# The first modulation third of a mixed attention, recurrence and expert layer, computed in two column halves

## The reference, cut to what matters

```python
def _modulation(cond, w, b):
    m = jax.nn.silu(cond) @ w + b
    return jnp.split(m[:, None, :], 6, axis=-1)

def _modulate(x, g, shift, scale):
    return _rmsnorm(x, g) * (1.0 + scale) + shift

proj = h @ p['w_in']          # h: the modulated x, 1024 features; w_in: 3232 columns
```

## Time and profile before

| | |
|---|---|
| three timed runs | 1644.02, 1645.7 and 1647.08 us; median 1645.7 |
| profiled execution, its own time | 1647.82 us |
| span of the profiled execution | 1646.0 us |
| granted TensorE clock, mean over the span | 0.956 of full |
| PE busy | 1508.4 us (92%) |
| DVE, ACT busy | 567.3 and 252.2 us |
| layer 1 starts (first ada product) | 839.23 us |
| DMA | 548.91 MB, mean 333 GB/s |

### The profile page before, as it was taken

The page is one execution under the profiler, slowest core; times in us unless marked ns, Lnnn a source line. Parts: engine busy times, 40 slices in busy tenths (PEclk is TensorE's granted clock), DMA queues, the critical chain, the costliest instruction groups (busy, mean ns, idle before and its releaser), DMA issues.

```text
span 1646.0 us, 19838 instructions
## 1 busy us (share of the span) xinstructions
PE 1508.4 (92%) x8048; PEld 886.4 (54%) x8048; DVE 567.3 (34%) x1463; ACT 252.2 (15%) x567; POOL 31.7 (2%) x30
## 2 busy tenths in 40 slices
PE   6999999989999989686899999999899999897878
PEld 2755788774454434242348567887744544343333
DVE  2368335435521112010144782363446112111112
ACT  2044122121000001000030442220200000000001
POOL 0000010020000000000000000100200000000000
PEclk7999999989999989798999999999899999999989
DMA  9743714787999999999996447228789999999995
GB/s 395 267 170 147 311 60 185 289 350 319 390 431 430 430 431 429 431 431 426 426 427 246 163 153 307 90 116 348 323 342 390 432 429 430 431 430 430 431 425 248
DMA packets 55914, 548.91 MB, mean 333 GB/s; under 512 B 13576, under 2 KB 14600, under 8 KB 21008
## 3 DMA queue, kind: packets, MB, share of 16 engines
q1 hardware_dynamic: 46416, 543.11, 79.2%
q10 hardware_dynamic: 9408, 4.53, 1.0%
HBM read 545.21 MB, written 2.42 MB: 333 GB/s over the span
## 4 chain that ended last, share of the span: by engine, by line
PE 74%; DMA 15%; DVE 6%; SPq 3%; issue 1%; ACT 0%; ACTq 0%; DVEq 0%
PE ps L782 19%; PE ps L1019 14%; PE ps L1049 10%; DMA arena<-exp_w_dram 8%; PE ps L743 7%; DMA ring<-exp_w_dram 5%; PE ps L960 5%; PE ps L1060 4%; PE ps L749 3%; PE ps L653 2%; SPq L484 2%; DMA ring<-front_dram 1%; PE ps L719 1%; PE ps L968 1%; PE ps L714 1%; PE ps L680 1%
## 5 line engine op out<-in xcount | busy, mean ns | idle before, releaser
L1019 PE MATMUL ps<-ring,arena 128*32 128x512 f32 (+2 forms) x1216 | 297.1, 628 | 41.9 <-DMA arena<-exp_w_dram 26.0
L1019 PE MATMUL ps<-arena 128*64 128x512 f32 (+1 forms) x896 | 231.9, 615 | 12.4 <-DMA ring<-exp_w_dram 12.4
L1019 PEld LDWEIGHTS ps<-ring,arena 128*32 128x32 f32 (+2 forms) x1216 | 90.4, 132 | 202.5 <-issue 194.6
L782 PE MATMUL ps<-hT,ring 128*128 128x256 f32 x768 | 171.4, 379 | 0.0
L1049 PE MATMUL ps<-ring,arena 128*32 128x512 f32 (+1 forms) x704 | 146.4, 622 | 16.8 <-DMA ring<-exp_w_dram 16.8
L782 PEld LDWEIGHTS ps<-hT,ring 128*128 128x128 f32 x768 | 144.1, 190 | 19.4 <-issue 1.0
L782 PE MATMUL ps<-arena,ring 128*128 128x256 f32 x640 | 147.0, 381 | 2.9 <-ACT arena L1243 1.6
L960 PE MATMUL ps<-arena,hT 128*128 128x128 f32 x896 | 120.6, 292 | 14.5 <-DVE arena L1755 14.5
L960 PEld LDWEIGHTS ps<-arena,hT 128*128 128x128 f32 x896 | 113.3, 205 | 35.7 <-DVE arena L1755 18.3
L782 PEld LDWEIGHTS ps<-arena,ring 128*128 128x128 f32 x640 | 117.8, 190 | 19.3 <-issue 2.7
L1019 PEld LDWEIGHTS ps<-arena 128*64 128x64 f32 (+1 forms) x896 | 67.5, 128 | 106.8 <-issue 106.8
(11 more groups left out here) (294 smaller groups left out, 1387.8 us busy)
## 6 DMA issues: line engine op xcount, KB each, us to landing
ring<-exp_w_dram SPq DMA_DIRECT2D x104, 2048.0 KB, 22.9
arena<-exp_w_dram SPq DMA_DIRECT2D x63, 2048.0 KB, 22.9
ring<-front_dram SPq DMA_DIRECT2D x58, 2048.0 KB, 10.3
arena<-exp_w_dram SPq DMA_DIRECT2D x24, 1024.0 KB, 29.1
ring<-exp_w_dram SPq DMA_DIRECT2D x16, 1024.0 KB, 13.7
ring<-exp_w_dram SPq DMA_DIRECT2D x24, 512.0 KB, 15.0
arena<-exp_w_dram SPq DMA_DIRECT2D x8, 512.0 KB, 29.5
ring<-front_dram SPq DMA_DIRECT2D x2, 1152.0 KB, 20.7
```

The costliest lines, as they stand in the source:

```text
L782: last = mm(out, slot[:, k, cols], src[:, k, :], start=k == 0, stop=k == nk - 1)
L1019: last = mm(ps[c, h, :], xTg[:, 4 * part + k, c], w[i][k][:, h * 512:(h + 1) * 512], start=False, stop=True, skip_group_check=True)
```

## The change

The first third is computed in two column halves. Half 0 takes columns 0 to 255 of each of the four groups of 512, half 1 columns 256 to 511. For shift and scale alike these are feature chunks 0, 1, 4, 5 and 2, 3, 6, 7, so everything that follows takes the chunks in the order `H_ORDER`. Each half has its own bank (0 and 1), its own copy on ACT (256 columns), its own two transposes (banks 3 and 4) and its own bias and `A1` operations on DVE.

In layer 0 PE takes each arriving ada block for both halves, then both pairs of transposes. In layer 1 PE does half 0 of all eight chunks, then the norm, the transposes of half 0, half 1 of all eight chunks, and then starts the input products; the transposes of half 1 stand inside unit 0, ahead of its third chunk. `ada_mm`, which frees the ring slots, is now raised by the products of half 1 alone.

On DVE the scaling and modulating of chunks alternate in layer 1, and the eight small operations come after all modulation. On ACT the softplus of layer 1 comes after the modulation. Two semaphores are merged and the counts adjusted.

```diff
+H_ORDER = (0, 1, 4, 5, 2, 3, 6, 7)
...
-                            sp_.wait_ge(*nth(ada_sb, 2, l))
+                            sp_.wait_ge(*nth(ada_sb, 3, l))
...
+                    def first_ada_products(half, slots):
+
+                        for k in (k for n in slots for k in (2 * n, 2 * n + 1)):
+                            slot = arrived(pe, l, S_ADA[0] + k // 2).rearrange("p (k n) -> p k n", k=2)
+                            for j in range(4):
+                                c = slice(j * 512 + half * 256, j * 512 + half * 256 + 256)
+                                last = mm(ps[32 * j:32 * j + 32, half, 0:256], cT[:, k, :], slot[:, k % 2, c],
+                                          start=k == 0, stop=k == KC - 1)
+                            if half and k % 2:
+                                last.then_inc(ada_mm, 1)
+                            if half == 0 and k == KC - 1:
+                                last.then_inc(ada_half, 1)
+
+                    def first_ada_transposes(half):
+                        pe.wait_ge(*nth(ada_sb, half + 1, l))
+                        for b in range(2):
+                            c = slice(half * 256 + b * P, half * 256 + (b + 1) * P)
+                            last = tr(ps[:, 3 + half, b * P:(b + 1) * P], msb[0][:, c], ident)
+                        last.then_inc(ada_tr, 1)
...
                     if l:
-                        ada_products(0, 0, range(KC // 2))
+                        first_ada_products(0, range(4))
                         norm(2)
-                        ada_products(0, 0, range(KC // 2, KC))
+                        first_ada_transposes(0)
+                        first_ada_products(1, range(4))
                     else:
                         norm(2)
                         pe.wait_ge(s_set[3], 4)
-                        ada_products(0, 0)
-                    ada_transposes(0, 3)
+                        for n in range(4):
+                            for half in range(2):
+                                first_ada_products(half, (n,))
+                        first_ada_transposes(0)
+                        first_ada_transposes(1)
...
-                                for k in range(KC):
+                                for i, k in enumerate(H_ORDER):
                                     if u == 0:
-                                        pe.wait_ge(*nth(h_v, k + 1, l))
+                                        if l and i == 2:
+                                            first_ada_transposes(1)
+                                        pe.wait_ge(*nth(h_v, i + 1, l))
...
+                    def first_modulation(half):
+                        if half == 0:
+                            act.wait_ge(*nth(ada_half, 1, l))
+                        else:
+                            act.wait_ge(*nth(ada_mm, 4, l))
+                        A(msb[0][:, half * 256:half * 256 + 256], ps[:, half, 0:256], ACT.Copy).then_inc(ada_sb, 1)
+
+                    def softplus():
+                        act.wait_ge(*nth(sp_abs, 1, l))
+                        link(A(sp[:, 8:16], sp[:, 0:8], ACT.Exp, scale=-1.0))
+                        A(sp[:, 16:24], sp[:, 8:16], ACT.Ln, bias=one_col).then_inc(ln_exp, 1)
+
+                    if l:
+                        first_modulation(0)
                     act.wait_ge(*nth(nrm_mm, 1, l))
                     A(rs[:, :], ps[:, 2, 0:NT], ACT.Sqrt, bias=cst[:, C_EPS:C_EPS + 1],
                       scale=1.0 / D).then_inc(nrm_sq, 1)
...
+                    if l == 0:
+                        softplus()
+                        first_modulation(0)
+                    first_modulation(1)
...
-                    for k in range(KC):
-                        act.wait_ge(*nth(hraw, k + 1, l))
+                    for i, k in enumerate(H_ORDER):
+                        act.wait_ge(*nth(mod_rdy, 1 + i // 4, l))
+                        act.wait_ge(*nth(hraw, i + 1, l))
...
+                    if l:
+                        softplus()
...
+                    if l:
+                        first_modulation(0)
                     dve.wait_ge(*nth(nrm_sq, 1, l))
                     link(V.reciprocal(rs[:, :], rs[:, :]))
-                    for k in range(KC):
-                        V.tensor_tensor(hT[:, k, :], xT[:, k, :], rs[:, :], ALU.mult).then_inc(hraw, 1)
-
+                    if l:
+                        scaled_x(H_ORDER[0])
+                        for i in range(4):
+                            scaled_x(H_ORDER[i + 1])
+                            modulate(i)
+                        for k in H_ORDER[5:]:
+                            scaled_x(k)
+                    else:
+                        for k in H_ORDER:
+                            scaled_x(k)
+                        first_modulation(0)
+                        for i in range(4):
+                            modulate(i)
+                    first_modulation(1)
+                    for i in range(4, 8):
+                        modulate(i)
```

More of the change, by code:

```diff
@@ L1372, in rsqrt, with modulation @@
                                                         op0=ALU.add, op1=ALU.mult))
+                    def modulation(r, bank):
+                        dve.wait_ge(*nth(ada_tr, r + 2, l))
+                        src = ps[:, bank, :].rearrange("p (b j z) -> p j b z", b=4, j=4)[:, :, :, 0:G]
+                        dst = modT[:, 16 * r:16 * r + 16, :].rearrange("p (j b) z -> p j b z", j=4)
+                        bias = vec[:, V_ADAB + 16 * r:V_ADAB + 16 * r + 16].rearrange("p (j b) -> p j b", j=4)
+                        link(V.tensor_tensor(dst, src, bias[:, :, :, None].broadcast_to((P, 4, 4, G)), ALU.add))
+                        if r == 1:
+                            V.tensor_scalar(g1h[:, :, :], modT[:, 16:24, :], 0.5, None, ALU.mult).then_inc(mod_rdy, 1)
+                        else:
+                            V.scalar_tensor_tensor(out=A2[:, :, :], in0=modT[:, 32:40, :], scalar=1.0,
+                                                   in1=vec[:, V_N2:V_N2 + 8][:, :, None].broadcast_to((P, KC, G)),
+                                                   op0=ALU.add, op1=ALU.mult).then_inc(mod_rdy, 1)
@@ new lines, in first_modulation @@
+                    def first_modulation(half):
+                        dve.wait_ge(*nth(ada_tr, half + 1, l))
+                        b = slice(2 * half, 2 * half + 2)
+                        src = ps[:, 3 + half, 0:256].rearrange("p (b j z) -> p j b z", b=2, j=4)[:, :, :, 0:G]
+                        dst = modT[:, 0:16, :].rearrange("p (j b) z -> p j b z", j=4)
+                        bias = vec[:, V_ADAB:V_ADAB + 16].rearrange("p (j b) -> p j b", j=4)[:, :, b]
+                        link(V.tensor_tensor(dst[:, :, b, :], src, bias[:, :, :, None].broadcast_to((P, 4, 2, G)), ALU.add))
+                        for j in range(2):
+                            k = 4 * j + 2 * half
+                            last = V.scalar_tensor_tensor(
+                                out=A1[:, k:k + 2, :], in0=modT[:, 8 + k:10 + k, :], scalar=1.0,
+                                in1=vec[:, V_N1 + k:V_N1 + k + 2][:, :, None].broadcast_to((P, 2, G)), op0=ALU.add,
+                                op1=ALU.mult)
+                        last.then_inc(mod_rdy, 1)
```

81 lines of the change are left out of this document (33 added, 48 removed).

## The result

The changed kernel takes 1650.33 us (median of 8 runs, 1649.18 to 1653.96), the kernel before 1646.34 (8 runs, 1643.61 to 1647.44): ratio 1.0025, 95% interval 1.0016 to 1.0035. It is slower by 4.0 us where +1.7 was forecast. The profiled execution took 1653.96 us, its span is 1652.1; it is the slowest of the eight, 3.6 us above their median.

A forecast was written before the change was run, and what follows sets the result against it. PE was taken to bound the kernel (three quarters of the chain), then DMA, saturated between layers. Terms -1.1 - 1.15 + 1.45 + 2.5 = +1.7 on 1645.7 gave 1647.4 us, no measurable change; range 1644.3 to 1650.0.

The forecast's parts named there:

- Layer 0, the start: Layer 0's start: last ada block lands at 28.5 either way, first input product at 33.9 against 35.00, -1.1 us.
- Layer 0, the clock: Layer 0's start: shorter PE idle time brings the full clock back at about 36.4 instead of 39.8, -1.15 us.
- middle: Layer 0's clock rise taken at about 36.4, between staying at 39.8 and coming before 33.9.
- Layer 1, the wait: Layer 1's ada products: PE waits 3.9 us for block 3, so the norm ends at 850.85, 4.4 us late.
- Layer 1, what is given back: Layer 1, after the norm: small operations leave the path, first input product at 855.1 against 853.68, net +1.45 us.
- the tie of DVE and PE: Layer 1's start: DVE allows the first input product at 854.8, PE's half 1 ends at 854.7.
- Layer 1, the clock: Layer 1, behind the wait for block 3: the clock falls to half rate, costing +2.5 us.
- Between: From layer 0's start on: PE has no hole worth the name until the experts, so a shift passes on; 0 us.
- the late blocks hidden: Layer 1: blocks 6 to 9 issued later, block 6 landing by about 865, needed at 873 or later; no cost.
- the signs named in the prediction: Among them: layer 0's first input product at 33.9; layer 1's 1 to 4 us later, counted from first ada product.
- the second one's other way: Slower side of the narrow-products rival: layer 0's clock gives nothing, layer 1's costs 2.85 us; chance 0.13 with that rival.
- The clock doesn't fall in layer 1: Rival for layer 1's start: clock stays full despite the wait; net -0.85 us, 1644.9 us, chance 0.10.

The follow-up runs named there:

- e2: Changed kernel with layer 1's order undone (blocks 0 and 1 for both halves, norm, blocks 2 and 3), halves kept: 1644.58 us, ratio 0.9995.
- b1: Kernel before with only the first third's products issued 256 columns wide, into two banks, order unchanged: 1650.77 us, ratio 1.0027.
- e3: Changed kernel with layer 1's norm moved between blocks 1 and 2 of half 0: 1646.33 us, ratio 0.9997.
- g3: g2 plus unread filler products of 512 columns where PE waits at the starts of both layers: 1650.55 us, ratio 1.0031.
- g4: g3 with fewer fillers, each of 256 columns: 1642.2 us, ratio 0.9973.
- e1: Changed kernel with nine unread products put on PE just ahead of layer 1's wait for block 3: 1648.67 us, ratio 1.0011.
- a1: Changed kernel, nothing altered, a third profile: 1651.48 us.
- g2: Kernel before with DVE's small operations moved behind the modulation, and in layer 1 ACT's softplus too; no products split: 1643.96 us, ratio 0.9988.
- p1: Kernel before, nothing altered, one more profile: 1647.89 us.

## Why the prediction was wrong

The means of the table's rows (four profiles of before, three of after) split the difference: to unit 4 of layer 0 54.93 and 55.38, +0.45; to layer 1 783.44 and 785.61, +2.2; layer 1's start 34.79 and 37.14, +2.35; the rest 773.20 and 773.17, nothing. Together +4.95 in these profiles, +4.0 in the medians of the timed runs. The forecast had -2.3, 0, +3.95, 0.

**Layer 0, the start: -1.1 forecast.** The step that failed is its first sentence, "the last ada block lands at 28.5 ... either way". The path behind the landing got shorter by 1.17 (forecast 1.1). But the block lands 1.5 us later, at 29.9 to 30.3 in all three profiles of the changed kernel and in both of e2 and of b1 (e3: 29.7). I had costed the 64 further products by their time on PE alone, which is nothing, and not as instructions that must themselves be loaded by the engines that carry the ring's blocks (the rows of queue 8 above: 3.0% of the 16 engines' time in those 2 us). b1, which adds only these products, has the earlier transfer and the later landing. g3, with 20 further products, has the transfer at 32.8, and there block 3 lands at 28.9 as before and block 4 is the late one (34.8 in place of 33.3); g4, with 13, has it at 36.6, behind blocks 3 and 4, which both land as before (28.5 and 33.4). Blocks 3 to 5 shift with it; from block 6 on the two kernels' blocks land alike (block 6 at 41.3 in both), since before has its transfer, and a like gap, ahead of that one. In layer 0 the link is one of place and time in every kernel looked at; that the transfer itself takes up 1.5 us of the stream, 0.02 MB though it is, was not isolated, and in layer 1 the link doesn't hold every time (below).

**Layer 0, the clock: -1.15 forecast.** Not obtained. The first 64 input products took 20.0, 20.1 and 20.3 us in the changed kernel and 20.7, 21.0, 20.0 and 20.0 before, so 0.3 on the mean. My "middle" between two ends had no row behind it. The clock there takes either way in like kernels: 18.35 in e1 and e2, 20.01 in e3.

**Layer 1, the wait: forecast 0.45 and 3.9 us,** norm's end 11.6 us behind the first ada product (839.23 to 850.85). Measured 1.77 and 3.79, norm's end at 15.6 (841.18 to 856.79). Of the 4.0 more, 1.5 is block 3, which PE takes up 8.56 us behind the first ada product in place of 7.04; 2.5 is the clock, which I booked in a term of its own. This delay, too, goes with the longer program and not with the order: block 3 lands 7.0 to 7.1 us behind the first ada product in all eight profiles without narrow products, and 7.3 to 8.6 in the nine with them (b1: 7.6 and 8.5). On queue 8, two instruction transfers stand at about 821 and 841 us in the changed kernel and in b1, where before has one, at 829.5 to 831.4. The one at 841 is not the cause: the blocks land 4.8 to 4.9 us apart across it, PE takes up blocks 2 and 3 at 844.88 and 849.74, and block 0 has the whole delay already. Its issue and its time to landing, first before, then after:

```profile
801.95 4.21 SPq L434 DMA_DIRECT2D ring<-front_dram  x1
DMA to landing us min/median/max: 29.8/29.8/29.8
```

```profile
803.89 4.21 SPq L435 DMA_DIRECT2D ring<-front_dram  x1
DMA to landing us min/median/max: 31.3/31.3/31.3
```

So it lands 7.5 us ahead of the first ada product before and 6.0 after. The cause lies earlier in the stream, possibly at 821, which no run isolates. In a1 the transfers stand at the same places with only 0.3 us of delay, so in layer 1 the price is between 0.3 and 1.5 and what sets it is open.

**Layer 1, what is given back: 3.95 us from norm's end to first product.** Measured 3.74 (856.79 to 860.53); the tie of DVE and PE was seen rightly, the transposes inside unit 0 add 0.24 (forecast 0.3). (By the forecast's own terms half 1 starts at 851.3 and not at 851.1, which moves its sum by 0.1.) What remains of a gain in layer 1 needs no halves: with the eight small operations out of the way g2 has its first input product 13.24 and 13.51 us behind the first ada product, and e2 and e3, which have the halves as well, have 13.30, 13.41 and 13.43.

**Layer 1, the clock: +2.5 forecast.** Measured against the shown profile: 0.87 on the half chunks and 1.46 on the norm, 2.3, and 2.1 by e1. The Trainium skill, "TensorE: Matmul & The Clock Gate", last section, blames idle gaps between bursts. The trace agrees here: the clock is 0.50 behind the wait of 3.79 us. But the start of before, which I read as free of this, has the low clock in three of its four profiles, for 2.9 us. Part 1 of the same page of the Trainium skill says, of a kernel's start, that the number of slow products varies from run to run of the same kernel. These profiles show such a variation in the middle of one, 18.32 against 21.2 us for the same 64 products; the earlier trace rows were one execution and could not show it. So the true difference in layer 1's start is 2.35, less than forecast and not more.

**Between: 0 forecast, +2.2 measured.** I had said that PE runs without a hole worth the name and that a shift passes on unchanged. The changed kernel loses 0.4 to 0.7 between 179 and 303 us, and 0.8 to 1.3 and 1.0 to 1.2 around two gathers of layer 0's experts. One gather before (first row) and after:

```profile
455.15 4.49 PE L960 MATMUL ps<-arena,hT 128*128 128x128 f32 x24 [3.74 <-DVE arena L1755]
```

```profile
456.54 5.49 PE L987 MATMUL ps<-arena,hT 128*128 128x128 f32 x24 [3.75 <-DVE arena L1830]
```

The same wait, the same work, 1.0 us longer at low clock. The other gather is 5.84 before and 6.76 after. Such losses stand in one of b1's two profiles, in e1, in e3 and in e2's first too, so they come with the longer programs more often than not and not with the order. The second gather takes 5.39 in g3 as well, with its 20 further products, and 4.4 to 4.5 in before and g2. What decides them was not found. So of the 4.95 us in these profiles, 2.2 have no known cause.

**What held:** the new wait (3.9 us forecast, 3.79 measured) and its place, the low clock behind it, the late blocks hidden, softplus and small loads hidden, narrow products half as long. Of the signs named in the prediction two failed: the first input product of layer 0 came at 35.38 and not at 33.9, and that of layer 1 came 4.9 us later than before, counted from the first ada product (19.35), and not 1 to 4. Of the rivals none came out as written; the second one's other way (layer 0's clock gives nothing, layer 1's costs 2.85) came half true, with 0.3 and 2.3. "The clock doesn't fall in layer 1" is refuted for the changed kernel (three profiles of three), and e1, where it doesn't fall, has 1648.67 and not the rival's 1644.9.

In the profiles the miss is 3.3 us (+4.95 against +1.65): two gains in layer 0 that weren't there (2.75) and a middle that wasn't free (2.2), less 1.6 because the reference for layer 1 was too good (its start had the full clock, as one profile of before in four has). In the medians it is 2.9 (1650.3 against 1647.4): 2.3 in the difference between the kernels, and 0.6 because the kernel before has 1646.34 over eight runs, not 1645.7. That the error in the reference is of the other sign is luck: it hid a third of the other two (1.6 of 4.95). The wait for block 3 came out to 0.1 us although blocks 2 and 3 were both 1.5 us late, because the wait for block 2 took up the lateness (1.77 in place of 0.45).

## What to carry to other kernels

Before work is moved ahead in PE's order, set when each of its operands lands against when it would now be needed; where the stream is full, the last operand sets the place, and one step (here the norm) left ahead of it covers the wait (e3). Splitting products costs nothing on PE here (64 narrow records take 3.66 us, 32 wide ones 3.64), but it lengthens the program, and its instruction transfers move about in the same stream that carries the weights; look where they lie against the blocks that PE waits for. Read the clock from several profiles before it enters a sum, and look first for small work on the path that can simply go later (g2), then for idle times at a start that harmless products can fill, measured first and shorter than the hole (g4).

## What was not expected of the hardware

- One instruction transfer of 0.02 MB inside the ring's stream goes, in layer 0, with a gap between two landings of 6.0 to 6.4 us in place of 4.8 to 4.9: at 27 to 28 us, before block 3, in nine profiles of the longer programs, and at 32.8, before block 4, in g3 (in the four of before at 38 to 39, before block 6, with 6.2 to 6.5). In layer 1 it goes either way: in the shown profile of before a transfer at 850.2 stands in such a gap (blocks 3 and 4 land at 846.3 and 852.7), while one at 848.4 in p1 and one at 841.5 in the changed kernel leave 4.8 to 4.9 us between the landings.
- The granted clock fell to half after idle times of 0.72 and 2.2 us in three executions of before, and stayed at 1.00 in a fourth and in both of b1, with the same work ahead of it. It fell after 0.72 and 1.00 in g2's first profile and stayed after 0.72 and 1.28 in its second. The waits of 3.8 us lowered it every time, the one of 1.31 us in e3 did not.
- A product of 128x512 in float32 with a 128x128 stationary leaves two records and takes 0.9 us at full clock (6 products, 12 records, in 5.42). Four with 32 stationary columns each, side by side, take 0.96 for all four (8 products, 16 records, in 1.92).
